# Attention opening: the samples' cached values are issued without waiting for the prompt's local values to land

## The reference

```python
DIL_PATTERNS = ((128, 1), (512, 4), (2048, 16))     # window, stride of a head group
HEADS_PER_GROUP, HEAD_DIM = 8, 64

def attend(q_blk, rows):                            # one head group
    idx = rows[:, None] - steps[None, :]            # steps = arange(n_keys) * dilation
    s = einsum('bqhd,bqkhd->bhqk', q_blk, kg) + bias
    s = where(valid, s, NEG)
    lse = logsumexp(s)
    o = einsum('bhqk,bqkhd->bqhd', exp(s - lse), vg)
    return o, lse
# three groups, their outputs weighted by softmax of their lse, then @ w_o
```

## Time and profile before

| | us |
|---|---|
| median of 3 runs | 2118.76 (2118.57 to 2120.33) |
| profiled execution | 2118.12 |
| its span | 2116.4 |
| PE busy | 2063.5 |
| DVE busy | 1423.8 |
| ACT busy | 866.7 |
| POOL busy | 222.3 |

### The profile page before, as it was taken

How to read it: one execution, slowest core, us unless ns; L and a number is a source line. 1 busy time by engine, 2 the same in 40 slices (tenths; PEclk the granted TensorE clock), 3 DMA queues, 4 the chain that set the end, 5 groups by cost and what they waited for, 6 DMA issues and landing times.

```text
span 2116.4 us, 43514 instructions
## 1 busy us (share of the span) xinstructions
PE 2063.5 (97%) x16575; PEld 2003.1 (95%) x16575; DVE 1423.8 (67%) x2370; ACT 866.7 (41%) x1529; POOL 222.3 (11%) x269
## 2 busy tenths in 40 slices
PE   7999999999999999999999999999989999999998
PEld 7999999999999999999999999999987789999997
DVE  4583896594896498378738946247747588738945
ACT  3342353363553255246424533322234546424533
POOL 0000001304100000310000022021105110000022
PEclk9999999999999999999999999999998999999998
DMA  5243433222233233324433333467669423323331
GB/s 146 83 123 88 127 120 109 68 80 84 80 96 102 83 94 103 92 71 135 134 91 95 99 96 95 143 214 260 220 219 329 135 86 91 104 85 90 99 96 56
DMA packets 381762, 249.87 MB, mean 118 GB/s; under 512 B 10679, under 2 KB 363295, under 8 KB 381583
## 3 DMA queue, kind: packets, MB, share of 16 engines
q1 hardware_dynamic: 371271, 210.00, 33.3%
q0 software_dynamic: 10352, 37.95, 5.2%
HBM read 230.63 MB, written 22.35 MB: 120 GB/s over the span
## 4 chain that ended last, share of the span: by engine, by line
PE 82%; DVE 10%; ACT 3%; DMA 2%; issue 2%; SPq 0%; DVEq 0%; ACTq 0%
PE pair L813 37%; PE pair L946 32%; PE pair L853 5%; PE pair L1094 3%; DVE t_w_sum L2069 1%; DVE t_w_seven L2074 1%; DVE t_w_lo L1952 1%; PE pair L825 1%; PE pair L1210 1%; DVE t_u_sum L2378 1%; DMA t_w_raw<-in_attn_w_kv 1%; PE pair L1343 1%; DMA t_w_raw<-in_ffn_w 1%; DVE t_x_diff_lo L2046 1%; DVE t_stream L2300 1%
## 5 line engine op out<-in xcount | busy, mean ns | idle before, releaser
L946 PE MATMUL pair<-t_x_diff_hi,t_w_seven 128*128 128x272 f32 x1960 | 409.9, 289 | 0.0
L1483 ACT ACTIVATE t_w_hi<-t_w_raw 128x1024 fp32r<-128x1024 f32 (+2 forms) x138 | 161.7, 1174 | 395.1 <-PE pair L813 346.7
L946 PEld LDWEIGHTS pair<-t_x_diff_hi,t_w_seven 128*128 128x128 f32 x1960 | 320.3, 188 | 0.0
L1952 DVE TENSOR_TENSOR t_w_lo<-t_w_raw,t_w_hi 128x1024 fp32r<-128x1024 f32 (+2 forms) x138 | 210.1, 1522 | 142.7 <-ACT t_w_hi L1483 137.3
L946 PE MATMUL pair<-t_x_hi,t_w_seven 128*128 128x272 f32 x1120 | 240.1, 294 | 4.8 <-DVE t_c L2078 3.4
L946 PE MATMUL pair<-t_x_diff_lo,t_w_seven 128*128 128x272 f32 x840 | 241.7, 288 | 0.0
L813 PE MATMUL pair<-t_h_lo,t_w_hi 128*128 128x272 f32 x1144 | 236.5, 288 | 0.0
L813 PE MATMUL pair<-t_h_hi,t_w_lo 128*128 128x272 f32 x1144 | 236.4, 288 | 0.0
L813 PE MATMUL pair<-t_h_hi,t_w_hi 128*128 128x272 f32 x1144 | 236.3, 288 | 0.0
L946 PEld LDWEIGHTS pair<-t_x_hi,t_w_seven 128*128 128x128 f32 x1120 | 184.5, 188 | 15.6 <-issue 11.6
L813 PEld LDWEIGHTS pair<-t_h_hi,t_w_lo 128*128 128x128 f32 x1144 | 179.4, 188 | 0.0
(11 more groups left out here) (344 smaller groups left out, 5197.1 us busy)
## 6 DMA issues: line engine op xcount, KB each, us to landing
t_w_raw<-in_ffn_w SPq DMA_DIRECT2D x280, 256.0 KB, 3.1
t_w_raw<-in_ffn_w SPq DMA_DIRECT2D x64, 704.0 KB, 4.6
t_w_raw<-in_ffn_w SPq DMA_DIRECT2D x36, 512.0 KB, 3.8
t_cached<-in_cache_kv_w POOLq DMA_DIRECT2D x16, 1024.0 KB, 9.0
t_cached_v<-in_cache_kv_w POOLq DMA_DIRECT2D x32, 512.0 KB, 6.8
t_w_raw<-in_attn_w_kv SPq DMA_DIRECT2D x24, 512.0 KB, 3.9
t_w_raw<-in_attn_w_q SPq DMA_DIRECT2D x12, 512.0 KB, 4.0
scratch_bias_rows<-scratch_bias_row SPq DMA_DIRECT2D x12, 384.0 KB
```

The source lines that it names most:

```text
L946: m = nc.tensor.matmul(out[:, 0:HALF], w[:, k, :], b, start=start and k == 0 and j == 0, stop=k == 3 and j == 2, skip_group_check=not start)
L1483: nc.scalar.activation(whi[s][:, 0:KT[stage], :], raw[s][:, 0:KT[stage], :], ACT.Copy) \
L1952: nc.vector.tensor_tensor(lo[:, 0:k, :], raw[s][:, 0:k, :], hi[:, 0:k, :].bitcast(F32), ALU.subtract).then_inc(lo_made[s], 1)
```

## The change

GpSimd no longer waits for `v0_in` (the landing of the prompt's local values) ahead of its first loads of the samples' cached values. The other waits ahead of them stay, and so does TensorE's own wait for `v0_in`. No instruction but this wait is removed, added or moved.

```diff
@@ -2712,7 +2712,6 @@
                     load_keys(2 * n + s, s)
             for s in range(2):
                 pool.wait_ge(w_used[s], USED["wo"])
-            pool.wait_ge(v0_in, 16)
             pool.wait_ge(kq_used, (NCK - 1) * DEC_B)
             pool.wait_ge(srow_t, 1)
             pool.wait_ge(srow_ok, 1)
```

## The result

The changed kernel takes 2130.83 us (median of 5 runs, 2126.63 to 2131.15) against 2118.9 (5 runs, 2118.57 to 2120.62): a ratio of 1.0046, 95% interval 1.0034 to 1.0058. A second comparison on another occasion gave 2129.97 against 2119.96, 1.0045 (1.0031 to 1.0059). By the two comparisons the change costs 10 to 12 us.

What follows compares the result with a forecast made beforehand. The chain through TensorE was taken to bound the kernel, with no gain from the removed wait. b12's delay +9.2, L2502 -0.5 and clock +0.6 made +9.3 on 2118.76, so 2128.1 us, range 2122.0 to 2133.2.

Steps and rivals of the forecast that it cites:

- the likeliest case: Bias load b12 on SyncE's queue lands late behind GpSimd's mixed-in transfers and delays the chain, +5 to +12 us; chance 0.70.
- GpSimd's wake-up and first issue: GpSimd's first cached-value load follows VectorE's L2519 by 0 to 0.63 us, at 1576.0, 10.7 us earlier.
- b12 untouched behind the issue for: SyncE's queue keeps full rate until 1578.3, then half rate until 1579.3, before the queues alternate.
- packets then one to one: DMA engines take one packet from each queue in turn, so SyncE's moves 86.5 packets a microsecond instead of 598.
- b12's delay: The bias load that VectorE's L2556 waits for lands +9.2 us later, ends +4.5 to +13.7.
- prompt's values land, after L1288: The prompt's values that TensorE's L1373 reads land between 1603.4 and 1605.4, from 9.4 MB at the engines' measured rate.
- floor by them at L1373: Minimum loss from late prompt's values at TensorE's L1373, even if b12 is hardly touched: 5.1 to 7.1 us.
- L2502 undisturbed: VectorE's copy L2502, slow under GpSimd's issues, runs free of them: -0.5 us.
- clock: TensorE's granted clock may return one pair of heads later after the longer first pause: +0.6 us (0 to 1.2).
- wait for values at L1373: TensorE's L1373 has no wait for the prompt's values, which land in time behind a chain 9.2 us late.
- from L1343 on a constant: Sign of being right: everything from TensorE's L1343 on is shifted by a constant.
- the first rival: b12 gets through nearly whole and TensorE waits at L1373 for the prompt's values instead: +5.6 us, 2124.4; chance 0.10.

Runs made afterwards that it cites:

- after: The changed kernel (GpSimd's wait for v0_in removed) against the kernel before, its first profiled execution; 2130.83 us against 2118.9, ratio 1.0046.
- e8: The changed kernel measured again with nothing altered, against the kernel before; 2129.97 us against 2119.96, ratio 1.0045.
- e2: Against the kernel before, only part 0 of the cached values (3.1 MB) issued early, part 1 keeps the old wait; 2123.23 us against 2118.73, ratio 1.0027.
- e3: The changed kernel with transposes of the identity (10, 22, 45) added in TensorE's pauses, against the kernel before; 2128.59 us against 2118.73, ratio 1.0045.
- e9: The changed kernel with b12's loads moved ahead of the last key/value stores in SyncE's queue, against the kernel before; 2128.84 us, ratio 1.0038.
- e1: Against the kernel before, GpSimd's first value loads wait for b12 instead of the local values; 2119.26 us against 2118.73, ratio 1.0004.
- e10: GpSimd's first value loads wait for b12 instead of the local values, measured again against the kernel before; 2122.1 us against 2119.21, ratio 1.0014.
- before: The kernel without the change, GpSimd still waiting for the local values; 2118.9 us in the first comparison, 2119.96 in the second.
- e5: The kernel before with b12's loads moved ahead in SyncE's queue, against the kernel before; 2119.55 us against 2119.96, ratio 0.9997.
- The runs with fill: Transposes of the identity added in TensorE's pauses: changed kernel 2128.59 us, kernel before 2119.76, kernel before with b12 moved ahead 2120.01.
- e6: The kernel before with b12's loads moved ahead and transposes (13, 20) around the first scores, against the kernel before; 2120.01 us against 2119.21, ratio 0.9998.
- e7: Against the kernel before, GpSimd's first cached-value loads wait for all of the prompt's values, so start later; 2125.4 us against 2119.96, ratio 1.0027.
- e4: The kernel before with transposes of the identity (10, 22, 6) added in TensorE's pauses, against the kernel before; 2119.76 us, ratio 1.0004.

## Why the prediction was right, and where it was not

The forecast was 2128.1 us (+9.3), with a range of 2122.0 to 2133.2; measured were 2130.83 and 2129.97, about +10 to +12. Sign and size hold. That the size came out so near is in part luck: the likeliest case had b12 carry the loss, and what carried it was the wait for the prompt's values, which stood in the text as a floor and as a rival of chance 0.10. A term that was too large covered that one and a clock term that was too small.

| step of the prediction | forecast | measured |
|---|---|---|
| GpSimd's wake-up and first issue | 0 to 0.63 us, issue 10.7 us earlier | 0.62 us, 10.2 earlier (15.6 to 5.4) |
| b12 untouched behind the issue for | 2.3 us, then 1 us at half rate | 3.6 us, then 186 packets in 1 us, under a third |
| packets then one to one | yes, 86.5 a microsecond | yes, about 72 with 2 KB packets |
| b12's delay | +9.2 (+4.5 to +13.7) | +4.6 after, -0.7 e8, +5.5 e2, +8.2 e3 |
| prompt's values land, after L1288 | 32.4 to 34.4 | 33.9 after, 33.8 e8, 33.0 e9, 36.0 e3 |
| floor by them at L1373 | +5.1 to +7.1 | +6.9 |
| L2502 undisturbed | -0.5 | -0.4 |
| clock | +0.6 (0 to +1.2) | +2.9 after, +2.2 e8, +3.1 e9 |
| wait for values at L1373 | none | 2.3 after, 7.0 e8, 7.9 e9, 2.8 e3 |
| from L1343 on a constant | yes | yes, within 0.3 us |

**Right: nothing gained, and the turns of the queues.** The removed wait gave nothing, as no step of the path waited for cached values. The earlier transfers took turns with SyncE's packets one for one, as in the earlier trace rows, so a queue with short rows loses most of its rate. The Trainium skill (DMA: Bandwidth & Descriptors, "Queues, rings and completion order") has packets of typically 9 to 17 descriptors drained in turn; the turns are seen here, but a turn of SyncE's queue carries a single row, 0.5 KB for b12 and 2 KB for the prompt's values, against 3.6 KB of GpSimd's on average.

**Mis-sized: b12's term.** It was +9.2 us in the sum and measured +4.6. The step that failed is the start of the mixing and its half-rate stretch. I had moved by 10.7 us and put the mixing at 2.3 to 3.3 us behind the issue; it came 3.6 us behind it, which is 1.3 us more of 610 packets a microsecond, and more of b12 was through. The start of mixing isn't a constant either: b12 landed anywhere between 10.1 and 19.0 in the executions of the changed kernel and its close kin (e8, e3). GpSimd's first packet moves at 8.7 us after L1288 in after and at 9.1 in e8. In these 0.4 us some 250 packets of b12 get through at 610 a microsecond; at 70 a microsecond they need some 3.5 us, most of the 5.2 us between the two landings (an estimate from these rates). A term that is the difference of two nearly equal times, when b12 ends and when mixing begins, carries the scatter of both. The text had its ends at +4.5 and +13.7, and even these don't hold e8.

**Wrong: which wait binds.** The forecast case said that L1373 has no wait; it has one in all four profiles in which all 5.2 MB are issued early (after, e8, e9, e3). That is the first rival, to which I gave 0.10. The floor was worked out right (5.1 to 7.1, measured 6.9): it needs only the sum of bytes and the rate of the engines, whatever b12 does. It holds on one condition that the text didn't name, that the prompt's values are the last to get through. So it was in after, where the last cached value landed at 30.7 and the last of the prompt's at 33.9; not so in e1 (37.0 and 29.8), and there the loss at L1373 is 2.8 us. The fault was to give this case a small chance because a larger term of poor precision lay above it.

**Wrong: the clock.** I priced the return of the clock at the first pause only. The rival's wait brings a second pause, at L1373, and the clock stayed low 13.6 us longer. The price of it is read between L1373 and L1343: 7.6 us with that pause (6.9 in e8, 7.8 in e9 and e3, 6.8 in e1, 7.2 in e10), and 4.7 without it in before, e2 and e5. That is 2.9 us: 6.9 of wait, 2.9 of clock and 0.3 behind L1343 are the measured 10.1, where the first rival's own sum had only 5.6. The runs with fill were meant to show this apart and didn't: the pause as the cause rests on these profiles with it and without it, and on e8, which up to L1373 differs from before by the wait alone, not on an edit of the pause. And a pause isn't the only thing that goes with a low clock there: in e6 it was low over L1373 with no wait ahead of it.

**The advice that speaks for the change.** The Trainium skill (DMA: Bandwidth & Descriptors, "Rules for kernel authors") says to issue a DMA early and wait late. Here the early transfer had nothing left to hide, and e1, e2, e7 and the change itself give the price by how much is issued and when: +0.5 to +2.9 us with all of it behind b12, +4.5 with 3.1 MB of it ahead of b12's landing, +10 to +12 with all 5.2 MB there, and +5.4 when it comes too late.

**What stays open.** Why the profiled executions of e1 and e10 lose 4.4 and 5.3 us and the medians only 0.5 and 2.9; what sets the start of GpSimd's data behind an issue when SyncE's queue is full; what besides the pause brings the clock down in e4 and e6; and the 3.0 us that arise before 80 us.

## What to carry to other kernels

A wait ahead of a bulk transfer that nobody is short of can be a gate that keeps the engines free for a load that somebody needs: before removing it, list all that the other queues hold at the new issue time, with packet sizes and who waits for each. Work out the floor by bytes first (everything that must have landed, divided by the measured rate), and only then terms that hang on the order of two close events. Ask under which order of the queues the floor holds (6.9 us here with the issue at 5.4, 2.8 with it at 10.9), and if it holds in the likeliest order, give it the larger chance. A wait that it causes can cost more than its own length, here 2.2 to 3.1 us of low clock. And look on both sides: here 4.9 us later cost 5.4 us, since the moved loads had only 2.3 us (part 0) and 0.8 us (part 1) to spare.

## What the runs showed of the hardware that was not expected

- GpSimd's data begins late behind an issue while SyncE's queue is full. Its first packet moves 3.3 us behind the first issue in after and e8, 2.1 in before, and anywhere from 1.8 (e3) to 3.9 (e6, e10); where SyncE's queue was empty, in e7, it is 1.3 us, as with idle engines in the kernel before (issue at 1378.84, first packet at 1380.18).
- The granted clock can fall while TensorE is busy: in e4 at 1585.3, after 7.00 of 7 us busy, and it stayed at 0.50 with 8.78 of 10 us busy; in e6 at 1585.9, after 10.45 of 12, and stayed so over 11.51 of 13. Both times it falls during the 24 small products L1328 (32x64). No run here separates the size of the instructions from the pauses, so the reason stays open.
- Two executions of the same program differ by over 5 us in when one load lands (b12 in after and e8), and the time doesn't show it, as another wait takes it up. A single profile of such a kernel easily names the wrong wait as the cause: after's list puts 6.6 us at b12 and 2.3 at L1373, e8's 0.9 and 7.0.
